# Delta-rule mixer: three input groups of the short convolution as twelve exact fp32 tiles inside the delta stages

## The reference, cut to what matters

```
qkv, z, a, b, b_gate, c_gate, hs = split(h @ w_in)        # h is (512, 1024) after an RMS norm
qkv = silu(causal_dwconv(qkv, qkv_conv))                  # 4 taps
q, k, v = 8 heads of 64
g = -exp(a_log) * softplus(a + dt_bias); beta = sigmoid(b)
o = gated_delta_rule_chunked(l2_normalize(q), l2_normalize(k), v, g, beta)
y_a = rms_norm(o, o_norm) * silu(z)
y_b = b_gate * causal_dwconv(c_gate * hs, sc_conv)        # 3 taps
x = x + concatenate([y_a, y_b]) @ w_out
```

## Time and profile before

| what | value |
|---|---|
| median of three executions | 2445.48 us |
| profiled execution, whole | 2448.71 us |
| its span, first to last instruction | 2446.9 us |
| mean granted TensorE clock | 0.946 |
| TensorE busy | 2286.8 us (93%) |
| VectorE, ScalarE, GpSimd busy | 989.5, 735.1, 179.4 us |
| the mixer's projection | from 933.7 to 1102.4 us of the span |
| delta stages up to the output projection's first matmul | 1102.4 to 1283.2 us |

### The profile page before, as it was taken

How to read it: one execution, slowest core, us unless ns; L and a number is a source line. 1 busy time by engine, 2 the same in 40 slices (tenths; PEclk the granted TensorE clock), 3 DMA queues, 4 the chain that set the end, 5 groups by cost and what they waited for, 6 DMA issues and landing times. The chain is left out here.

```text
span 2446.9 us, 30512 instructions
## 1 busy us (share of the span) xinstructions
PE 2286.8 (93%) x12894; PEld 1744.6 (71%) x12894; DVE 989.5 (40%) x1682; ACT 735.1 (30%) x1214; POOL 179.4 (7%) x198
## 2 busy tenths in 40 slices
PE   6999999889999999997489999999998989999997
PEld 3545655768888877887467888887876667888885
DVE  3022266433333324944423432433236663432433
ACT  2124311222322223324222332332113663332331
POOL 0003200000000000002000000000214550000000
PEclk8999999799999998998569999999998999999999
DMA  7150012212132221200011222211420002222210
GB/s 309 45 222 35 1 42 97 106 69 79 77 115 109 78 79 69 104 35 1 1 70 69 103 77 96 103 72 71 138 104 35 2 1 104 103 75 98 104 69 35
DMA packets 17111, 195.84 MB, mean 80 GB/s; under 512 B 2000, under 2 KB 3152, under 8 KB 5072
## 3 DMA queue, kind: packets, MB, share of 16 engines
q1 hardware_dynamic: 15824, 189.67, 20.8%
q10 hardware_dynamic: 1152, 4.23, 0.4%
HBM read 189.70 MB, written 2.10 MB: 78 GB/s over the span
## 5 line engine op out<-in xcount | busy, mean ns | idle before, releaser
L1723 DVE TENSOR_TENSOR wsp_mlp<-ring,wsp_mlp 128x1024 fp32r<-128x1024 f32 x128 | 156.9, 1226 | 438.2 <-ACT wsp_mlp L1685 438.2
L1685 ACT CAST wsp_mlp<-ring 128x1024 fp32r<-128x1024 f32 x128 | 134.3, 1049 | 349.4 <-PE psum L1670 344.9
L1667 PE MATMUL psum<-hs_mlp,wsp_mlp 128*128 128x512 f32 x512 | 201.8, 394 | 8.1 <-DVE hs_mlp L1556 8.1
L1667 PE MATMUL psum<-acts_mlp,wsp_mlp 128*128 128x512 f32 x512 | 202.4, 395 | 0.0
L1669 PE MATMUL psum<-hs_mlp,wsp_mlp 128*128 128x512 f32 x512 | 201.3, 393 | 0.0
L1670 PE MATMUL psum<-hs_mlp,wsp_mlp 128*128 128x512 f32 x512 | 201.1, 393 | 0.0
L1669 PE MATMUL psum<-acts_mlp,wsp_mlp 128*128 128x512 f32 x512 | 199.2, 389 | 0.0
L1670 PE MATMUL psum<-acts_mlp,wsp_mlp 128*128 128x512 f32 x512 | 199.2, 389 | 0.0
L1723 DVE TENSOR_TENSOR wsp_ffn<-ring,wsp_ffn 128x1024 fp32r<-128x1024 f32 x66 | 80.9, 1226 | 237.3 <-ACT wsp_ffn L1685 237.3
L431 PE MATMUL psum<-hsev,wspev 128*128 128x512 f32 x672 | 157.3, 397 | 3.9 <-DVE wspev L411 3.9
L431 PEld LDWEIGHTS psum<-hsev,wspev 128*128 128x128 f32 x672 | 129.0, 192 | 31.9 <-DVE wspev L411 4.7
(11 more groups left out here) (429 smaller groups left out, 3865.0 us busy)
## 6 DMA issues: line engine op xcount, KB each, us to landing
ring<-weights SPq DMA_DIRECT2D x85, 2048.0 KB, 8.2
ring<-weights SPq DMA_DIRECT2D x3, 1024.0 KB, 5.1
xT<-xin SPq DMA_DIRECT2D x2, 1024.0 KB, 6.7
cst<-consts ACTq DMA_DIRECT2D x1, 1841.0 KB, 13.9
ring<-weights SPq DMA_DIRECT2D x1, 1280.0 KB, 5.4
mixT<-ctxin ACTq DMA_DIRECT2D x1, 1024.0 KB, 15.0
ring<-weights SPq DMA_DIRECT2D x2, 512.0 KB, 3.3
hT<-arena_low SPq DMA_DIRECT2D x8, 128.0 KB, 2.4
```

Source lines behind the costliest of these rows:

```text
L1667: pe.matmul(tile_bank(g, j), w_hi, src[:, 0, k0 + i, :], start=(first and i == 0), stop=False)
L1685: act.copy(wsp[:, q % 2, 0, :], raw_view(q)).then_inc(s["w_hi"], 1)
L1723: dve.tensor_tensor(wsp[:, q % 2, 1, :], raw_view(q), wsp[:, q % 2, 0, :].bitcast(F32), ALU.subtract).then_inc(s["w_lo"], 1)
```

## The change

- The plan of weights puts the two empty slots of the delta stages (`delta0`, `delta1`) ahead of `ev6`.
- The split projection covers `ev0` to `ev3` only, 16 units. `ev4`, `ev5`, `ev6` become twelve tiles of eight fp32 matmuls each (`sc_tile`), from ring weights that ScalarE scales in place by the norm's gain (`sc_scale`, eight operations of 128x512 to a group) and from `xT`, which already carries its own factor; the remaining factor `inv_r` is applied after the convolution.
- The work of the lengths block moves into the projection's block: gate sums and squares' sums run between units 14 and 15, the rest after unit 15. Tiles 0 and 1 run there.
- Products block: tiles 2 and 3 in halves of four matmuls after each pair of heads, in bank 7; the decay rows rotate over three banks.
- Inverse block: tiles 4 to 7 at its start, copied by ScalarE; VectorE multiplies and convolves between its steps.
- u/w block: ScalarE scales `ev6` after its last copy, VectorE convolves.
- Scan: tile 8 in pairs of matmuls ahead of each wait for VectorE's subtraction and at the end.
- Output norm: written out in a block of its own, with tile 9 around the sums and tiles 10 and 11 after the spread, each gated by VectorE.

```diff
     out += [(f"hg{i}", SLOT) for i in range(3)] + [(f"mod{i}", SLOT) for i in range(8, 12)]
     out += [(f"out{i}", SLOT) for i in range(2)]
     out += ffn_plan("gu", FFN1_UP, "dn", FFN1_DOWN)
-    out += [("ev_ab", 8 * 16)] + [(f"ev{i}", SLOT) for i in range(7)]
-    out += [("delta0", 0), ("delta1", 0)]
+    out += [("ev_ab", 8 * 16)] + [(f"ev{i}", SLOT) for i in range(6)]
+    out += [("delta0", 0), ("delta1", 0), ("ev6", SLOT)]
     out += [(f"evo{i}", SLOT) for i in range(2)]
     out += ffn_plan("up0_", MLP_UP, "down0_", MLP_DOWN)
...
-        high, low, unit, group_done = split_products([f"ev{g}" for g in range(7)], xT, hs, wsp, gain=ev_gain, flip=flip)
+        high, low, unit, group_done = split_products([f"ev{g}" for g in range(4)], xT, hs, wsp, gain=ev_gain, flip=flip)
+        sc_done, sc_out, sc_gain, x_scaled = sem("sc_done"), sem("sc_out"), sem("sc_gain"), sem("x_scaled")
+        sc_slot = []
+        for g in (4, 5):
+            sc_slot.append(claim(f"ev{g}"))
+            used(sc_done, 4 * (g - 3))
+        space_free = sem("space_free")
+        spare = []
+        for name in ("delta0", "delta1"):
+            spare.append(claim(name) % RING)
+            used(space_free, 1)
+        sc_slot.append(claim("ev6"))
+        used(sc_done, 12)
+
+        def sc_weights(m):
+            return ring[:, sc_slot[m // 4] % RING, :].rearrange("p (k n) -> p k n", k=KD)
+
+        def sc_tile(pe, m, out, steps=range(KD)):
+
+            for k in steps:
+                if k == 0:
+                    pe.wait_ge(sc_gain, KD * (m // 4) + KD)
+                last = pe.matmul(out, sc_weights(m)[:, k, (m % 4) * P:(m % 4) * P + P], xT[:, k, :], start=(k == 0),
+                                 stop=(k == KD - 1))
+            if k == KD - 1:
+                last.then_inc(sc_done, 1)
+
+        def sc_scale(act, g, ks):
+
+            if ks[0] == 0:
+                act.wait_ge(weight_landed[sc_slot[g] % RING], landed(sc_slot[g]))
+            for k in ks:
+                view = sc_weights(4 * g)[:, k, :]
+                act.mul(view, view, V("mix0", k, 1)).then_inc(sc_gain, 1)
+
+        def sc_copy(act, m, src):
+
+            act.wait_ge(sc_done, m + 1)
+            act.copy((ch if m < 4 else cs)[:, m % 4, :], src).then_inc(sc_out, 1)
...
+        def sc_product(dve, link, i):
+
+            dve.wait_ge(sc_out, 5 + i)
+            link(dve.tensor_tensor(ch[:, i, :], ch[:, i, :], cs[:, i, :], ALU.mult))
+            link(dve.tensor_tensor(ch[:, i, :], ch[:, i, :], inv_h2[:, :], ALU.mult))
+
+        def sc_conv(dve, link, i):
+
+            conv(dve, link, cs[:, i, :], ch[:, i, :], lambda j: V("sc_conv", 3 * i + j, 1), 3, cg_out)
+            dve.wait_ge(cg_out, i + 1)
+            dve.tensor_tensor(cs[:, i, :], cs[:, i, :], inv_r[:, :], ALU.mult).then_inc(hs_out, 1)
+
+        def sc_gate(dve, i, src):
+
+            dve.wait_ge(sc_done, 9 + i)
+            dve.wait_ge(hs_out, i + 1)
+            dve.tensor_tensor(mixT[:, 4 + i, :], src, cs[:, i, :], ALU.mult)
...
+                    if q in (8, 12):
+                        pe.wait_ge(bank_out, q - 4)
+                    if q == 15:
+                        pe.wait_ge(g_set, 1)
+                        pe.wait_ge(bank_out, 10)
...
+                        last.then_inc(gc_done, 1)
+                        pe.wait_ge(len_sq, 8)
...
+                        last.then_inc(sum_done, 1)
                     unit(pe, q)
...
+                pe.wait_ge(inverted, 1)
+                pe.wait_ge(gc_read, 1)
+                pe.wait_ge(bank_out, 12)
+                for r in range(4):
+                    spread_row(r)
+                pe.wait_ge(x_scaled, KD)
+                pe.wait_ge(bank_out, 13)
+                sc_tile(pe, 0, tile(12))
+                pe.wait_ge(scaled, 4)
+                pe.wait_ge(bank_out, 16)
+                for c in range(3):
+                    turn_keys(c)
+                for r in range(4, 8):
+                    spread_row(r)
+                pe.wait_ge(sc_out, 1)
+                turn_keys(3)
+                pe.wait_ge(silu_set, 12)
+                for c in range(TT):
+                    pe.wait_ge(scaled, 5 + c)
+                    for j in range(4):
+                        last = pe.transpose(tile(8 + c)[:, j * P:(j + 1) * P], cv[:, 8 + j, c * P:(c + 1) * P], ident)
+                    last.then_inc(v_turn, 1)
+                pe.wait_ge(k_read, 1)
+                sc_tile(pe, 1, tile(13))
...
+                    if q in (11, 12):
+                        sc_scale(act, 0, range(4 * (q - 11), 4 * (q - 11) + 4))
+                    if q in (14, 15):
+                        sc_scale(act, 1, range(4 * (q - 14), 4 * (q - 14) + 4))
...
+                for i in range(4):
+                    act.wait_ge(bank_out, 13 + i)
+                    act.activation(mixT[:, i, :], mixT[:, i, :], ACT.Silu)
+                sc_copy(act, 0, tile(12))
+                act.wait_ge(v_turn, TT)
                 for c in range(TT):
-                    dve.wait_ge(k_turn, c + 1)
-                    k_t = bank(k_bank[c]).rearrange("p (h n) -> p h n", h=GH)
...
+                    if p == 2:
+                        pe.wait_ge(sc_out, 3)
+                    sc_tile(pe, 2 + p // 2, bank(7), range(4 * (p % 2), 4 * (p % 2) + 4))
...
+                    if h == 3:
+                        sc_copy(act, 2, bank(7))
+                sc_copy(act, 3, bank(7))
...
+                sc_product(dve, link, 0)
+                sc_product(dve, link, 1)
...
+                sc_conv(dve, link, 0)
...
+                sc_product(dve, link, 2)
+                sc_product(dve, link, 3)
...
+                for i in range(4):
+                    sc_copy(act, 4 + i, bank(4 + i))
...
+                for i in range(4):
+                    sc_tile(pe, 4 + i, bank(4 + i))
...
+                sc_scale(act, 2, range(KD))
...
+                    if p < 3:
+                        sc_conv(dve, link, p + 1)
...
+                        sc_tile(pe, 8, bank(3), range(2 * c - 2, 2 * c))
...
+                sc_tile(pe, 8, bank(3), range(6, 8))
...
+                sc_gate(dve, 0, bank(3))
...
+                for k in range(4):
+                    act.activation(hT[:, k, :], cv[:, 8 + k, :], ACT.Square).then_inc(o_sq, 1)
+                act.wait_ge(o_sum, 1)
+                act.activation(sums[:, 0:32], psum[:, 0:32], ACT.Sqrt, bias=epsc[:, 0:1], scale=1.0 / GD).then_inc(o_root, 1)
...
+                sc_tile(pe, 9, bank(5), range(0, 3))
+                for k in range(4):
+                    pe.wait_ge(o_sq, k + 1)
+                    for i in range(TT):
+                        at = 2 * (k * TT + i)
+                        last = pe.matmul(psum[:, at:at + 2], hT[:, k, i * P:(i + 1) * P], C("blk64")[:, 0:P:64],
+                                         start=True, stop=True)
+                last.then_inc(o_sum, 1)
+                sc_tile(pe, 9, bank(5), range(3, 8))
+                pe.wait_ge(o_inv, 1)
+                for k in range(4):
+                    for i in range(TT):
+                        at = 2 * (k * TT + i)
+                        for o in range(2):
+                            last = pe.matmul(bank(1 + k)[64 * o:64 * o + 64, i * P:(i + 1) * P],
+                                             rstd[:, at + o:at + o + 1].to_broadcast([P, 64]), ident,
+                                             start=True, stop=True)
+                    last.then_inc(o_row, 1)
+                sc_tile(pe, 10, bank(6))
+                sc_tile(pe, 11, bank(7))
+
+            @block.vector
+            def _(dve):
+                dve.wait_ge(o_root, 1)
+                dve.reciprocal(rstd[:, 0:32], sums[:, 0:32]).then_inc(o_inv, 1)
+                sc_gate(dve, 1, bank(5))
+                for k in range(4):
+                    dve.wait_ge(o_row, k + 1)
+                    dve.scalar_tensor_tensor(out=cv[:, 8 + k, :], in0=cv[:, 8 + k, :], scalar=V("o_norm"), in1=bank(1 + k),
+                                             op0=ALU.mult, op1=ALU.mult).then_inc(o_set, 1)
+                    dve.wait_ge(o_set, k + 1)
+                    dve.tensor_tensor(mixT[:, k, :], cv[:, 8 + k, :], mixT[:, k, :], ALU.mult)
+                sc_gate(dve, 2, bank(6))
+                sc_gate(dve, 3, bank(7))
```

More of the change, by code:

```diff
@@ new lines, in program, with blocks @@
+        grow = past[:, 0:2 * T].rearrange("p (a n) -> p a n", a=2)
+        edge = past[:, 2 * T:2 * T + 4 * TT].rearrange("p (a n) -> p a n", a=4)
+        vn = grow[:, 0, :].rearrange("p (h n) -> p h n", h=GH)
+        st = grow[:, 1, :].rearrange("p (b a n) -> p b a n", b=2, a=4)
+        mt = hT
+        NE = GH * TT
+        def blocks(ap, n):
+            return ap.rearrange("p (e n) -> p e n", n=n)
+        inner, lanes, rank1, xt32 = (ring[:, spare[0], 1024 * i:1024 * i + 1024] for i in range(4))
@@ L1841, in _ @@
                 last.then_inc(ab_done, 1)
-                for q in range(1, 28):
```

(58 more changed lines are left out.)

233 lines of the change are left out of this document (85 added, 148 removed).

## The result

The changed kernel took 2410.65 us (median of 4 runs, 2403.93 to 2414.34) where the kernel before took 2444.76 beside it: ratio 0.9857, 95% interval 0.9831 to 0.9884. The forecast was 2411.

What follows compares the result with a forecast made beforehand. TensorE was taken as the bound on the whole, at about half clock in parts of the delta stages. The terms sum to -34.3 us, from the median of 2445.48 to 2411 us; 8-in-10 range 2394 to 2425.

Steps and rivals of the forecast that it cites:

- Projection and lengths: From unit 14's end to the products block: twelve units go, lengths work and tiles 0 and 1 move in; gain 60.6 us.
- Products: Products block: half tiles stand ahead of the next pair's products, 10 of 13.9 us hide in the wait for ScalarE; +4.2.
- Inverse: Inverse's start: four tiles, 27.8 us at full clock, run under VectorE's 26.3 us chain; +1.4 us.
- u and w: End of u and w: ScalarE's eight scalings of ev6 stand exposed behind its last copy; +5.3 us.
- Scan: Scan: tile matmuls partly fill TensorE's waits, while dense matmuls lift the clock and give some 3.8 us back; +3 us.
- Output norm: Output norm: rest of tile 9, sums, spread rows, tiles 10 and 11 and the gate take 29.7 us; +13.6.
- Output projection: Output projection: starts after a TensorE gap of 4.6 us instead of 6.2, so may keep full clock; -1.2 us.
- A: Inverse, u and w, scan's start: clock stays full after the inverse's four tiles; 2394 us, chance 0.18.
- B: Scan and last block: tiles at half clock, or later handovers in the moved lengths work; 2423 us, chance 0.16.
- C: Products, inverse and last block: exact tiles run at half clock, each 6.94 us longer; slower, 2473 us, chance 0.04.
- D: Projection block: moved lengths work holds unit 15 by as much as is saved; span unchanged, 2445 us, chance 0.02.

Runs made afterwards that it cites:

- e4: Changed kernel with ev6's 2 MB transfer sent for in the block of u and w, after the 64x64 work, instead of in the inverse: 2410.27 us, ratio 0.9850.
- e3: Changed kernel with ScalarE's eight scalings of ev6 between its copies in u and w instead of behind the last: 2410.20 us, ratio 0.9855.
- e2: Changed kernel with only one of each exact tile's eight matmuls left, its inputs thus incomplete: 2383.46 us, ratio 0.9748.
- e6: Changed kernel with three of tile 9's last five matmuls among the output norm's sums instead of behind them: 2412.01 us, ratio 0.9852.
- e1: Kernel before without its twelve units for the short convolution's inputs, zeros in their place: 2385.82 us, ratio 0.9753.
- e7: Changed kernel with tile 7 moved from under VectorE's chain in the inverse, one matmul at a time, into the 64x64 work: 2431.56 us, ratio 0.9934.
- e9: Changed kernel with tile 0 among the squares' sums ahead of unit 15 instead of between the spread rows: 2421.05 us, ratio 0.9902.
- e8: Changed kernel with the edits of e3, e4 and e6, and the squares' sums among unit 15's matmuls: 2408.78 us, ratio 0.9836.
- e10: Changed kernel with the three edits of e3, e4 and e6 together: 2402.70 us, ratio 0.9822.
- e12: Changed kernel with the edits of e3, e4 and e6, and e9's tile 0 among the squares' sums: 2404.68 us, ratio 0.9839.

## Why the prediction was right, point by point

The time and the sign were right, 2410.65 against 2411, and so was the main mechanism: the twelve units' time goes, and the tiles hide where TensorE was idle. That the time was met within 1 us is luck: the stages' misses are +1.3, -2.0, -0.1, +1.7, -0.3, -3.7, +2.7 and +0.3, which nearly cancel. In one term, the scan, the mechanism was wrong.

- **Projection and lengths**, -60.6 forecast, -59.3 by stages; from unit 14's end 46.8 us against 44.8. The step that was mis-sized is the first: gate and squares' sums, 10.7 forecast, 13.35 measured. I had read 12 starts in a microsecond from the earlier trace rows, but a window counts instructions that straddle its edges, two or three of them here, so both rates were too high: 80 records in 14.9 us before (2.4 of them at full clock) and in 13.4 now (3.9 of them) give 9.3 a microsecond at full clock and 4.6 at half, not 12 and 6.2. Unit 15 took 7.6 (8.0), tiles 6.97 (6.9), turns and rows between them 7.3 (7.4), the handover 0.95 (1.1).
- **Products**, +4.2 forecast, +2.2 measured. The step that was mis-sized is its start. I took 2.85 and 2.8 us for the first decay rows and products, which are the prices of the kernel before, where the clock was mostly at half there; behind tile 1 the clock is at full and they take 1.95 and 1.98 from start to start, 1.7 us less. The three steps with a half tile took 7.40 each (7.58), 0.5 less in all. The first lines, changed kernel and then before:

```profile
1075.69 2.02 PE L2185 MATMUL psum<-cst,arena_low 128*128 128x128 f32 x16 [0.93 <-PEq L1938]
1077.64 2.06 PE L2196 MATMUL psum<-arena_low 64*128 64x128 f32 x32
1079.62 2.05 PE L2185 MATMUL psum<-cst,arena_low 128*128 128x128 f32 x16
```

```profile
1140.02 2.82 PE L2137 MATMUL psum<-arena_low 64*128 64x128 f32 x32
```

- **Inverse**, +1.4 forecast, and the chain's stage gave 1.3. The step "2 MB have the rest of the stage, over 20 us, to land" was incomplete: it asked whether the transfer comes in time, not what it does to its neighbours. It cost 1.7 to 2.0 us of TensorE's 32x32 work (e4), in a part of the stage that the forecast put at nothing.
- **u and w**, +5.3 forecast, +5.0 measured; "nothing hides it" is shown by e3, where moving it gives 5.0 back.
- **Scan**, +3 forecast, -0.7 measured. The step that failed is "the dense matmuls lift the clock". The tiles cost 3.7 (e2 against the changed kernel), not the 4.4 and 2 of the forecast. Without them the scan takes 20.7 against 25.1 before: 4.4 are given back by the clock, which is near the 3.8 that I had, but the tiles don't bring it. In the changed kernel the scan's first predict matmuls (L2467) already run at full clock, 1.13 us where the same sixteen took 1.97 before, and the first tile matmul stands behind them. In e2 the only tile matmul of the scan stands at its end, and the clock is 0.93 where before it was 0.64. The changed kernel, the kernel before, and the window of e2's scan:

```profile
1189.68 1.13 PE L2467 MATMUL psum<-cst,ring 64*128 64x64 f32 x16
1190.74 1.98 PE L1853 MATMUL psum<-xT,ring 128*128 128x512 f32 x4
```

```profile
1241.06 1.97 PE L2384 MATMUL psum<-arena,ring 64*128 64x64 f32 x16
```

```profile
1173.90:1194.60 20.70, 17.02 (x210) 11.37 (x210) 4.89 (x12) 2.35 (x5) 0.00 (x0) 0.93 0.20 74
```

  So this part of the term was met by luck, and with the late rise of e3 to e6 the term is about +2. Why the clock rose later before, with the same matmuls, stays open; e1, which has the scan of the kernel before, shows its 25.2 us and 0.64 again.
- **Output norm**, +13.6 forecast, +16.3 measured. Of the miss 2.0 is the rest of tile 9, 7.5 us against 4.3 and 1.2 for the clock: I let the clock come back too early. 0.9 is the sums, 3.9 against 3.0, the same counting as above. e6 shows that both go if the clock is held. (In e7 and e9 this stage had 34.4 and the output projection 48; it is not as steady as the others.)
- **Output projection**, -1.2 forecast, -0.9 measured.

**The rivals.** A (full clock through inverse, u and w) is refuted by the changed kernel's 0.50 there with TensorE busy 22.08 of 28 us, and again by e7. By that, the rule of the Trainium skill, "TensorE: Matmul & The Clock Gate", section "HAM oscillation — how this bites in real kernels", which asks for no idle gaps, is not enough here: e9's first window has TensorE busy 25.90 of 25.90 us at 0.58. B (half clock in the scan and in the last block) is half right: not in the scan of the changed kernel, though six of its variants had the clock at half for the first 8 us there, but in the last block, where e6 prices it at 3.4 us. C (tiles at half clock) would have been right for another placing: in e7 one tile moved into the 64x64 work cost 16.4 us net, and in e9 tile 0 among the sums cost 7.2 more than where the change puts it. D (no change) fell with the first stage.

## What to carry to other kernels

Work moved into another engine's chain is free only as far as TensorE idles there and as the clock is up: here 40 of 73 us were hidden, and the same matmuls cost next to nothing beside VectorE's chain (1.3 us for 24 us of matmuls), nearly their own length in the last block (15.8 us for 18), and twice that among small matmuls at half clock. Put wide matmuls in an unbroken run, where they bring the clock up, and keep them out of a long stretch of narrow ones; among the 32 narrow ones of the output norm, behind wide work, they were worth 3.4 us, among the 64 of the projection block they cost 7.2. Place the transfers and scalings that a moved step brings with it as carefully as the matmuls: two of them were worth 7 us by their stages and cost a few lines each.

## What the runs showed of the hardware that I had not expected

- The mixture of eight 2-column records (0.89 us) and two 128x512 records (0.87 us) holds 1.00 for 6 us in the output norm (e6, and again e8, e10 and e12) and stays at 0.50 for 21 us in the projection block (e9), TensorE busy throughout in both. What went before differs: tile matmuls in one, sixteen 8-column records in the other; no run shows that this is the reason. Unit 15's unbroken 128x512 matmuls then bring it back within some 4 us.
- The scan's clock rises some 3 us into it in five kernels with all their tiles and in e2, and some 8 us into it in six, over the same instructions; the scan is 24.4 to 24.9 or 26.9 to 27.5 us long by that.
- A 2 MB transfer of 8.6 us beside 32x32 matmuls goes with TensorE stalls without a visible releaser, 4.0 us against 2.5 without it, and the stage is 2.0 us longer.
- VectorE's 128x512 multiplications, 0.69 us alone, took 0.98 while GpSimd copied beside them (e4), and GpSimd's four copies 3.65. In e4's timeline, VectorE while GpSimd copies and after:

```profile
1137.89 0.98 DVE L1884 TENSOR_TENSOR mixT<-mixT,arena_low 128x512 f32<-128x512 f32 x1
1138.90 0.98 DVE L1885 TENSOR_TENSOR mixT<-mixT,arena_low 128x512 f32<-128x512 f32 x1
...
1152.35 0.69 DVE L1884 TENSOR_TENSOR mixT<-mixT,arena_low 128x512 f32<-128x512 f32 x1
```
